# Forgetting attention: the causal masks of the diagonal blocks added in PSUM by VectorE instead of by TensorE products

## The chip, the core and the metric

The kernel runs on one core of one Trainium2 chip. The metric is device time in microseconds (us) of one launch. Engines: TensorE (PE; its weight loads are PEld), VectorE (DVE), ScalarE (ACT), GpSimd (POOL) and SyncE (SP). They run their own queues of instructions and meet through semaphores.

## The reference, cut to what matters

The program computes a chain of layers on a sequence of 1024 positions with 1024 channels in float32. The change touches one of them, the forgetting attention with 16 heads of 64 channels:

```
c = cumsum(log_f)                       # per head
logits[t, s] = q_t . k_s / sqrt(64) + c[t] - c[s]
mask = s <= t
probs = softmax(where(mask, logits, -inf))
out = probs @ v
```

Of a block of 128 queries, only the block of keys with the same positions (the diagonal block, 128 x 128) is cut by the mask; the keys before it are all seen, those behind it are never computed.

## The kernel before

The heads are done two at a time, eight pairs (p). `act_fox_pair`, `pe_fox_pair` and `dve_fox_pair` hold a pair's work for each engine; seven pairs run as a hardware loop (`Fori`), the eighth stands behind it. Every operand of a matrix product is split in a high and a low fp32r part, so that exact products take two or three passes.

A pair has two kinds of phases.

**Maximum phase, once for each head r.** For the eight blocks i of queries, TensorE computes the scores against the keys up to and with block i (`score`, line 2086, one product for each 512 columns) into one of two pairs of PSUM banks of psA, and adds the mask of the diagonal block with one more product of 128 columns (line 2088: identity times FHIDE, a 128 x 128 matrix that is large where the key lies behind the query). VectorE (`peak`, line 2407) adds the row of c and takes the minimum over all columns in one instruction; a second one reads the accumulator (READ) into NMX. It needs `fs_full` from TensorE; TensorE's score i+2 needs `fmax_ready` of peak i. After eight peaks TensorE turns the maxima (`row`, line 2095), and ScalarE writes them into a row of FX2 (line 2274).

**Sums, both heads.** The turned scores (keys on partitions) come in 24 pieces j of up to 512 queries. `PIECES` gives for each (r, h, n): head, half of the queries and block of keys. Where n >= 4h the piece begins at its diagonal block; those are pieces 0 to 7, 12 to 15 and 20 to 23, with widths 512, 384, 256, 128. For piece j: TensorE `turned` (lines 2111, 2112, and 2114, the mask product of 128 columns); ScalarE `exp` (2281) and `high` (2288); VectorE `low` (2413); TensorE `weigh` (2127, 2128 need the high part, 2130 the low part). The bank of piece j is reused by piece j+2, so TensorE's order is weigh(j), turned(j+2). The sums come out beside their denominators; `divide` (2423 reciprocals of 128 columns, 2430 and 2432 two multiplications) is spread over VectorE's queue by the table `DIVIDE`: behind low(5) to low(7), low(9) to low(13) and low(17) to low(21).

TensorE's order is written by hand: between these steps it works through slices of the next pair's projections (lines 321 to 323, three products of 512 columns a slice, into psG). `FILL_MAX` and `FILL_SUM` say how many slices stand ahead of each step, mostly one. In the last pair (`FILL_MAX_LAST`, `FILL_SUM_LAST`) the slices belong to the output projection, there are none ahead of the first six scores of head 0, and VectorE has low parts of that projection (line 999) between its peaks. GpSimd splits the weight tiles (lines 308, 310) when TensorE begins a tile, four times a pair.

`link` makes VectorE wait for its own instruction just issued (semaphore dve_step).

## Time and profile before

| | us |
|---|---|
| median of 3 runs | 2299.39 (2299.27 to 2303.89) |
| profiled execution, its own time | 2300.81 |
| its span in the profile | 2299.0 |
| mean granted TensorE clock, share of full speed | 0.981 |
| TensorE / VectorE / ScalarE / GpSimd busy | 2187.5 / 1205.1 / 861.0 / 551.7 |
| forgetting attention: seven looped pairs | 83.8 each |

The profile lists instructions with start and duration in us. A busy TensorE is not TensorE at its peak: durations of its products overlap, so what one costs is read from the starts. A bracket behind a row tells how long the engine was idle before it and what released it.

### The profile page before, as it was taken

What the parts mean: (1) busy time and instruction counts of PE and PEld (TensorE: products, weight loads), DVE (VectorE), ACT (ScalarE), POOL (GpSimd) and SP (SyncE); (2) the same over time, 40 slices, a digit from 0 to 9 for tenths busy, and PEclk for the clock granted to TensorE, in tenths of its full rate; (3) what the DMA queues carried; (4) which work ended last, traced back from release to release, by engine and by line L of the source; (5) the groups of instructions that cost most, each with busy time, mean ns of one, the idle gap of its engine ahead of it and who ended that gap; (6) DMA issues with size and microseconds to landing.
All of it is one profiled execution on the core that took longest, in us unless ns stands there. A gap on an engine that the chain in (4) does not pass through costs nothing.

```text
span 2299.0 us, 29340 instructions
## 1 busy us (share of the span) xinstructions
PE 2187.5 (95%) x11216; PEld 1852.2 (81%) x11216; DVE 1205.1 (52%) x1525; ACT 861.0 (37%) x1321; POOL 551.7 (24%) x292
## 2 busy tenths in 40 slices
PE   4899999999999899999899979999999999999996
PEld 4678888988888788898778868888888888877885
DVE  6963332453443634333435463566666667667734
ACT  3136554112022343323323123446546546544311
POOL 1322221323432122222233322111111111111520
PEclk9999999999999899999999989999999999999998
DMA  8112212111441211111131121111111011013201
GB/s 341 55 46 74 73 64 81 49 46 47 157 155 38 98 46 37 37 37 37 37 147 46 37 101 56 38 49 40 39 55 46 27 55 55 18 46 111 73 19 73
DMA packets 36661, 154.60 MB, mean 67 GB/s; under 512 B 4161, under 2 KB 4161, under 8 KB 35810
## 3 DMA queue, kind: packets, MB, share of 16 engines
q1 hardware_dynamic: 23840, 93.52, 11.7%
q10 hardware_dynamic: 12738, 59.87, 7.4%
q8 instruction: 64, 1.05, 0.2%
q14 instruction: 19, 0.16, 0.0%
HBM read 128.15 MB, written 21.04 MB: 65 GB/s over the span
## 4 chain that ended last, share of the span: by engine, by line
PE 84%; DVE 10%; issue 3%; ACT 2%; DMA 0%; DVEq 0%; SPq 0%; ACTq 0%
PE psG L321 22%; PE psG L323 21%; PE psG L322 21%; PE psA L2130 2%; PE psA L2112 1%; PE psA L2111 1%; PE psA L2128 1%; PE psA L2127 1%; PE psA L2012 1%; PE psA L321 1%; PE psA L2086 1%; PE psA L323 1%; PE psA L322 1%; DVE M L1043 1%; PE psA L2095 1%
## 5 line engine op out<-in xcount | busy, mean ns | idle before, releaser
L321 PE MATMUL psG<-AH,WH 128*128 128x512 f32 x2092 | 849.5, 406 | 39.2 <-DVE AL L999 12.3
L322 PE MATMUL psG<-AL,WH 128*128 128x512 f32 x2092 | 823.8, 394 | 0.0
L323 PE MATMUL psG<-AH,WL 128*128 128x512 f32 x2092 | 823.5, 394 | 0.0
L308 POOL TENSOR_SCALAR WH<-RAW 128x1024 fp32r<-128x1024 f32 x144 | 165.9, 1152 | 1659.9 <-PE psG L321 1183.3
L321 PEld LDWEIGHTS psG<-AH,WH 128*128 128x128 f32 x2092 | 398.1, 190 | 121.1 <-issue 26.4
L323 PEld LDWEIGHTS psG<-AH,WL 128*128 128x128 f32 x2092 | 397.1, 190 | 87.1
L322 PEld LDWEIGHTS psG<-AL,WH 128*128 128x128 f32 x2092 | 398.8, 191 | 68.3
L310 POOL TENSOR_TENSOR WL<-RAW,WH 128x1024 fp32r<-128x1024 f32 x144 | 386.0, 2680 | 12.0
L2413 DVE TENSOR_TENSOR FTL<-PF,FTH 128x512 fp32r<-128x512 f32 x192 | 112.8, 587 | 118.7 <-ACT FTH L2288 115.6
L2281 ACT ACTIVATE PF<-psA,PB 128x512 f32<-128x512 f32 x192 | 111.5, 581 | 81.2 <-PE psA L2114 45.6
L2423 DVE RECIPROCAL FDR<-psA 64x128 f32<-64x128 f32 x128 | 118.1, 939 | 32.1 <-PE psA L2130 30.5
L2407 DVE CUSTOM_DVE_ANT_0 JUNK<-psA,CB 128x128 bf16<-128x128 f32 (+7 forms) x128 | 96.7, 757 | 52.8 <-PE psA L2088 50.5
L321 PE MATMUL psG<-WH,AH 128*128 128x256 f32 x384 | 109.0, 284 | 0.0
L323 PE MATMUL psG<-WH,AL 128*128 128x256 f32 x384 | 108.7, 283 | 0.0
L322 PE MATMUL psG<-WL,AH 128*128 128x256 f32 x384 | 108.6, 283 | 0.0
L2288 ACT ACTIVATE FTH<-PF 128x512 fp32r<-128x512 f32 x192 | 100.8, 525 | 6.1
L1006 DVE TENSOR_TENSOR RS<-RS,SQ 128x1024 f32<-128x1024 f32 x38 | 70.3, 1850 | 34.4 <-ACT SQ L725 33.2
L725 ACT ACTIVATE SQ<-X 128x1024 f32<-128x1024 f32 x35 | 37.1, 1061 | 124.9 <-DVE X L1775 71.7
L322 PEld LDWEIGHTS psG<-WL,AH 128*128 128x128 f32 x384 | 73.7, 192 | 0.0
L321 PEld LDWEIGHTS psG<-WH,AH 128*128 128x128 f32 x384 | 73.7, 192 | 0.0
L323 PEld LDWEIGHTS psG<-WH,AL 128*128 128x128 f32 x384 | 73.7, 192 | 0.0
L713 ACT ACTIVATE AH<-Y 128x1024 fp32r<-128x1024 f32 x32 | 32.5, 1054 | 96.8 <-PE psG L323 78.1
(358 smaller groups left out, 3042.5 us busy)
## 6 DMA issues: line engine op xcount, KB each, us to landing
RAW<-w_tiles SPq DMA_DIRECT2D x144, 512.0 KB, 3.5
gates<-SIG ACTq DMA_DIRECT2D x16, 512.0 KB, 2.9
park<-X ACTq DMA_DIRECT2D x2, 4096.0 KB, 11.5
CB<-fox_c ACTq DMA_DIRECT2D x16, 512.0 KB, 4.4
X<-xT SPq DMA_DIRECT2D x4, 1024.0 KB, 12.1
WADA_SCALE<-w_ada SPq DMA_DIRECT2D x1, 4096.0 KB, 24.0
WADA_SHIFT<-w_ada SPq DMA_DIRECT2D x1, 4096.0 KB, 34.1
WADA_GATE<-w_ada ACTq DMA_DIRECT2D x1, 4096.0 KB, 16.4
```

Source lines behind the costliest of these rows:

```text
L308: nc.gpsimd.tensor_scalar(WH[:, i, :], RAW[:, i % RAW_SLOTS, :], 1.0, 0.0, ALU.mult, ALU.add).then_inc(w_high, 1)
L310: nc.gpsimd.tensor_tensor(WL[:, i, :], RAW[:, i % RAW_SLOTS, :], WH[:, i, :].bitcast(F32), ALU.subtract).then_inc(w_split, 1)
L321: first = nc.tensor.matmul(out, wh, xh, start=start, stop=False)
L322: nc.tensor.matmul(out, wh, xl, start=False, stop=False)
L323: return first, nc.tensor.matmul(out, wl, xh, start=False, stop=stop)
L1006: nc.vector.tensor_tensor(RS[:, :], RS[:, :], SQ[:, j % 2, :], ALU.add).then_inc(sq_used, 1)
L2130: nc.tensor.matmul(out, FVH[:, n, vs], FTL[:, j % 2, 0:w], start=False, stop=j in ENDS).then_inc(fpv_done, 1)
L2281: nc.scalar.activation(PF[:, j % 2, 0:w], psA[:, j % 2, 0:w], ACT.Exp, bias=PB[:, n, r:r + 1], scale=-1.0).then_inc(fexp_done, 1)
L2288: nc.scalar.activation(FTH[:, j % 2, 0:w], PF[:, j % 2, 0:w], ACT.Copy).then_inc(ft_high, 1)
L2407: nc.vector.tensor_tensor_reduce(out=JUNK[:, s % 2, 0:n], in0=pair((i + 1) % 2)[:, 0:n], in1=CB[:, r, 0:n], scale=1.0, scalar=3e38, op0=AL ...
L2413: nc.vector.tensor_tensor(FTL[:, j % 2, 0:w], PF[:, j % 2, 0:w], FTH[:, j % 2, 0:w].bitcast(F32), ALU.subtract).then_inc(ft_ready, 1)
L2423: l = nc.vector.reciprocal(FDR[hs, cs], psA[ds, 2 + r, cs])
```

## The change

- The mask product leaves `score` and `turned` (before: lines 2087, 2088, 2113, 2114).
- In `peak`, VectorE adds FHIDE (now plain float32) in place to the diagonal block in PSUM, waits for that addition with `link`, increments peak_begun, and then runs the reduction.
- In the sums, a new step `own(j)` of VectorE adds FHT, the other orientation of the mask, in place to the first 128 columns of the pieces in `OWN` (the 16 with a diagonal block) and signals `ft_masked`, for which `exp(j)` now waits. own(0) and own(1) stand ahead of low(0); own(j+2) stands behind low(j) and the first division step of that place.
- FHT is made once by VectorE from a constant matrix. Two semaphores f_min and f_ready become one. `chain.loop` keeps the count of the links within the loop.

```diff
@@ score (TensorE)
-                last = ks.stop == n
-                l = nc.tensor.matmul(out, FX[:, r, i * P:n], FKA[:, r, ks], start=True, stop=not last)
-                if last:
-                    l = nc.tensor.matmul(psA[:, 2 * b + i // 4, (i % 4) * P:(i % 4 + 1) * P], IDR[:, :], FHIDE[:, :], start=False, stop=True)
+                l = nc.tensor.matmul(out, FX[:, r, i * P:n], FKA[:, r, ks], start=True, stop=True)
@@ turned (TensorE)
-            l = nc.tensor.matmul(out, FKB[:, r, ks], FX2[:, r, qs], start=False, stop=lo > n * P)
-            if lo == n * P:
-                l = nc.tensor.matmul(psA[:, j % 2, 0:P], FHIDE[:, :], IDR[:, :], start=False, stop=True)
-            l.then_inc(ft_full, 1)
+            nc.tensor.matmul(out, FKB[:, r, ks], FX2[:, r, qs], start=False, stop=True).then_inc(ft_full, 1)
@@ exp (ScalarE)
-            act.wait_ge(ft_full, p * N_P + (j + 1))
+            if j in OWN:
+                act.wait_ge(ft_masked, p * len(OWN) + (OWN.index(j) + 1))
+            else:
+                act.wait_ge(ft_full, p * N_P + (j + 1))
@@ peak and own (VectorE)
+            own = psA[:, 2 * ((i + 1) % 2) + i // 4, (i % 4) * P:(i % 4 + 1) * P]
+            link(nc.vector.tensor_tensor(own, own, FHIDE[:, :], ALU.add))
             dve.sem_inc(peak_begun, 1)
...
+        def own(j):
+            if j in OWN:
+                dve.wait_ge(ft_full, p * N_P + (j + 1))
+                nc.vector.tensor_tensor(psA[:, j % 2, 0:P], psA[:, j % 2, 0:P], FHT[:, :], ALU.add).then_inc(ft_masked, 1)
@@ the sums of a pair (VectorE)
+        own(0)
+        own(1)
         for j in range(N_P):
             low(j)
-            for step in DIVIDE.get(j, ()):
+            steps = DIVIDE.get(j, ())
+            for step in steps[:1]:
+                divide(*step)
+            own(j + 2)
+            for step in steps[1:]:
                 divide(*step)
```

VectorE in the maximum phase, head 0, peaks 5 and 6, before (ISA with JUNK is the reduction, ISA with NMX alone the READ; the increment of peak_begun is not shown in such rows):

```order
L2400 REGISTER_ALU
L2407 ISA JUNK,NMX<-psA,CB 128x768 [waits fs_full,fmax_ready]
L2407 ISA NMX 128x1
L2400 REGISTER_ALU
L2407 ISA JUNK,NMX<-psA,CB 128x896 [waits fs_full,fmax_ready]
L2407 ISA NMX 128x1
```

The same place after the change:

```order
L2401 REGISTER_ALU
L2407 TENSOR_TENSOR psA<-psA,FHIDE 128x128 [waits fmax_ready,fs_full]
L228 REGISTER_ALU
L2410 ISA JUNK,NMX<-psA,CB 128x768 [waits dve_step]
L2410 ISA NMX 128x1
L2401 REGISTER_ALU
L2407 TENSOR_TENSOR psA<-psA,FHIDE 128x128 [waits fmax_ready,fs_full]
L228 REGISTER_ALU
L2410 ISA JUNK,NMX<-psA,CB 128x896 [waits dve_step]
L2410 ISA NMX 128x1
```

Each peak has one more VectorE instruction, and the reduction waits for VectorE's own semaphore instead of TensorE's.

VectorE in the sums, after the change, from the end of step j = 4 to low(7); before the change the rows of line 2416 are not there:

```order
L2416 TENSOR_TENSOR psA<-psA,FHT 128x128 [waits ft_full]
L2421 TENSOR_TENSOR FTL<-PF,FTH 128x384 [waits ft_high]
L2431 RECIPROCAL FDR<-psA 64x128 [waits fpv_done]
L2415 REGISTER_ALU
L2416 TENSOR_TENSOR psA<-psA,FHT 128x128 [waits ft_full]
L2431 RECIPROCAL FDR<-psA 64x128
L2421 TENSOR_TENSOR FTL<-PF,FTH 128x256 [waits ft_high]
L2431 RECIPROCAL FDR<-psA 64x128 x2
L2421 TENSOR_TENSOR FTL<-PF,FTH 128x128 [waits ft_high]
```

The additions are own(6) and own(7); they wait for TensorE, and low(5) and low(6) stand behind them.

VectorE at the end of a diagonal, from own(14) to low(14), after the change:

```order
L2416 TENSOR_TENSOR psA<-psA,FHT 128x128 [waits ft_full]
L2421 TENSOR_TENSOR FTL<-PF,FTH 128x384 [waits ft_high]
L2437 REGISTER_ALU [waits psum_free]
L2438 ISA [waits fdr_ready]
L2438 TENSOR_TENSOR FDR<-FDR,Y 64x512
L2439 REGISTER_ALU
L2440 TENSOR_TENSOR Y<-psA,FDR 64x512 [waits fdr_ready]
L2415 REGISTER_ALU
L2416 TENSOR_TENSOR psA<-psA,FHT 128x128 [waits ft_full]
L2421 TENSOR_TENSOR FTL<-PF,FTH 128x256 [waits ft_high]
```

own(14) and own(15), the two additions, stand ahead of low(13) and low(14).

## Rows read from the trace of the kernel before

**Rows 1.** The page: TensorE's busy time (part 1), the reductions (part 5).

```profile
PE 2187.5 (95%) x11216; PEld 1852.2 (81%) x11216; DVE 1205.1 (52%) x1525; ACT 861.0 (37%) x1321; POOL 551.7 (24%) x292
...
L2407 DVE CUSTOM_DVE_ANT_0 JUNK<-psA,CB 128x128 bf16<-128x128 f32 (+7 forms) x128 | 96.7, 757 | 52.8 <-PE psA L2088 50.5
```

**Rows 2.** Windows: second maximum phase and sums; from:to, us, busy (instructions), clock, DMA.

```profile
1622.50:1633.60 11.10, 10.67 (x53) 8.37 (x52) 7.33 (x18) 0.89 (x2) 3.46 (x2) 1.00 0.00 0
1634.30:1680.80 46.50, 46.42 (x243) 39.63 (x242) 28.68 (x42) 32.76 (x59) 4.66 (x3) 1.00 0.07 23
```

**Rows 3.** Timeline of TensorE around a mask product; start us, duration us, engine, line, operation.

```profile
1655.58 0.39 PE L2112 MATMUL psA<-FX,FKB 128*128 128x512 f32 x1
1655.80 0.22 PE L2114 MATMUL psA<-IDR,FHIDE 128*128 128x128 f32 x1
1655.86 0.45 PE L321 MATMUL psG<-AH,WH 128*128 128x512 f32 x1
1656.14 0.39 PE L322 MATMUL psG<-AL,WH 128*128 128x512 f32 x1
```

**Rows 4.** Timeline of the maximum phase, head 0.

```profile
1613.40 0.39 PE L2086 MATMUL psA<-FKA,FX 128*128 128x512 f32 x1
...
1613.63 0.22 PE L2088 MATMUL psA<-FHIDE,IDR 128*128 128x128 f32 x1
...
1614.07 0.69 DVE L2407 CUSTOM_DVE_ANT_0 JUNK<-psA,CB 128x512 bf16<-128x512 f32 x1 [0.47 <-PE psA L2088]
...
1618.85 1.23 DVE L2407 CUSTOM_DVE_ANT_0 JUNK<-psA,CB 128x1024 bf16<-128x1024 f32 x1 [0.16 <-DVE NMX L2407]
...
1620.00 0.08 DVE L2407 DVE_READ_ACCUMULATOR2_ANT NMX<- 128x1 f32 x1
...
1620.14 1.09 PE L2095 MATMUL psA<-MATS,NMX 128*128 128x128 f32 x8
```

**Rows 5.** Timeline of VectorE in the maximum phase, head 1: first reduction, last READ.

```profile
1624.63 0.28 DVE L2407 CUSTOM_DVE_ANT_0 JUNK<-psA,CB 128x128 bf16<-128x128 f32 x1
...
1633.37 0.08 DVE L2407 DVE_READ_ACCUMULATOR2_ANT NMX<- 128x1 f32 x1
```

**Rows 6.** Timeline of VectorE: a division, each operation waiting for the one before.

```profile
1604.34 0.95 DVE L2423 RECIPROCAL FDR<-psA 64x128 f32<-64x128 f32 x1
1605.43 0.69 DVE L2430 TENSOR_TENSOR FDR<-FDR,Y 64x512 f32<-64x512 f32 x1
1606.16 0.69 DVE L2432 TENSOR_TENSOR Y<-psA,FDR 64x512 f32 x1
```

**Rows 7.** Timeline of the sums: low(14), low(15), last product of weigh(14).

```profile
1662.00 0.43 DVE L2413 TENSOR_TENSOR FTL<-PF,FTH 128x256 fp32r<-128x256 f32 x1
...
1663.02 0.29 DVE L2413 TENSOR_TENSOR FTL<-PF,FTH 128x128 fp32r<-128x128 f32 x1 [0.59 <-ACT FTH L2288]
1663.07 0.28 PE L2130 MATMUL psA<-FTL,FVH 128*128 128x256 f32 x1
```

**Rows 8.** Timelines: VectorE beside GpSimd's subtraction, in three places.

```profile
1571.78 1.69 DVE L2413 TENSOR_TENSOR FTL<-PF,FTH 128x512 fp32r<-128x512 f32 x1
...
1653.91 2.81 POOL L310 TENSOR_TENSOR WL<-RAW,WH 128x1024 fp32r<-128x1024 f32 x1
1655.58 1.69 DVE L2413 TENSOR_TENSOR FTL<-PF,FTH 128x512 fp32r<-128x512 f32 x1
...
2116.40 2.40 POOL L310 TENSOR_TENSOR WL<-RAW,WH 128x1024 fp32r<-128x1024 f32 x1
2117.59 2.58 DVE L1775 TENSOR_TENSOR X<-X,psG 128x1024 f32<-128x1024 f32 x2
```

**Rows 9.** The last pair: first reduction, READ of the fifth; window 2036 to 2042.

```profile
2030.11 0.29 DVE L2407 CUSTOM_DVE_ANT_0 JUNK<-psA,CB 128x128 bf16<-128x128 f32 x1 [0.24 <-PE psA L2088]
...
2033.44 0.08 DVE L2407 DVE_READ_ACCUMULATOR2_ANT NMX<- 128x1 f32 x1
...
2036.00:2042.00 6.00, 4.47 (x15) 3.39 (x13) 5.43 (x5) 3.24 (x4) 3.96 (x2) 0.75 0.11 33
```

More of the change, by code:

```diff
@@ L1868, in build @@
     LFT, NCT = sb("LFT", [P, NB, FOX_HEADS], 220), sb("NCT", [P, NB, FOX_HEADS], 220.5)
-    FHIDE = sb("FHIDE", [P, P], 221, F32R)
+    FHIDE, FHT = sb("FHIDE", [P, P], 221), sb("FHT", [P, P], 222.3125)
     FREC = sb("FREC", [P, 2, 2 * NB], 221.5)
@@ L1878, in build @@
     SUMS_AT = HALF - 4 * NB
+    OWN = [j for j, (r, h, n) in enumerate(PIECES) if n >= 4 * h]
     FILL_MAX = [0, 1, 1, 1, 1, 1, 1, 1, 2, 0, 1, 2, 1, 1, 1, 1, 1, 1, 2]
@@ L1891, in build @@
     assert Q_AT[0] > filled(16) and K_AT[0] > filled(32)
-    f_min = sem("f_min")
     f_log = sem("f_log")
@@ L1922, in build @@
     fexp_done = sem("fexp_done")
+    ft_masked = sem("ft_masked")
     ft_high = sem("ft_high")
@@ L2028, in pe_fox_in @@
         gemm(pe, *fox_tile(0, 1))
-        pe.wait_ge(f_ready, 1)
+        pe.wait_ge(f_ready, 2)
         for n in range(NB):
@@ L2034, in pe_fox_in @@
         l.then_inc(f_turned, 1)
-        pe.wait_ge(f_ready, 2)
+        pe.wait_ge(f_ready, 3)
         for n in range(NB):
@@ L2245, in act_fox_gates @@
         fs = slice(0, FOX_HEADS)
-        act.wait_ge(f_min, 1)
+        act.wait_ge(f_ready, 1)
         nc.scalar.activation(EXF[fs, :], unit(U_F % 2)[fs, :], ACT.Abs, bias=col("b_f")[fs, :]).then_inc(psum_free, 1)
@@ L2370, in dve_fox_gates @@
         dve.wait_ge(psum_full, U_F + 1)
-        nc.vector.tensor_scalar(LF[fs, :], unit(U_F % 2)[fs, :], col("b_f")[fs, :], 0.0, ALU.add, ALU.min).then_inc(f_min, 1)
-        dve.wait_ge(f_min, 1)
+        nc.vector.tensor_scalar(LF[fs, :], unit(U_F % 2)[fs, :], col("b_f")[fs, :], 0.0, ALU.add, ALU.min).then_inc(f_ready, 1)
+        dve.wait_ge(f_ready, 1)
         dve.wait_ge(f_log, 1)
@@ L2376, in dve_fox_gates @@
         nc.vector.tensor_copy(LFT[:, :, :].rearrange("p n h -> p (n h)"), psA[:, 0, 0:NB * FOX_HEADS]).then_inc(f_ready, 1)
+        nc.vector.tensor_scalar(FHT[:, :], mat("causal_sum"), NEG, -NEG, ALU.mult, ALU.add)
         for r in range(2):
@@ L2474, in dve_fox @@
         with dve.Fori(0, PAIRS - 1) as p:
+            chain.loop(p, N_S)
             dve_fox_pair(dve, p, True)
+        chain.done(PAIRS - 1)
+        chain.loop(0, N_S)
         dve_fox_pair(dve, PAIRS - 1, False)
+        chain.done(1)
     def dve_final(dve, k):
```

## The prediction

> **What bounds the kernel now.** I read the page first: TensorE is busy 2187.5 of 2299.0 us, 95%; the times of VectorE's reductions stand in the same page [rows 1]. So each product that leaves TensorE is worth its issue time, as long as nothing else becomes the last thing that TensorE waits for. That is read from the stages the change touches. Seven of the eight head pairs repeat with a period of 83.8 us (the same long subtraction starts at 1571.78 and at 1655.58 [rows 8]). In the pair I read, TensorE has 0.43 us without work in the second maximum phase and 0.08 us in the 46.5 us of the sums [rows 2]: it is full. The timelines then show who is next. In the maximum phase the last reduction of head 0 is followed by the turning of the maxima 0.06 us after it ends (READ 1620.00 + 0.08, TensorE 1620.14), and TensorE had nothing left before that: VectorE ends this phase already [rows 4]. In the sums VectorE hands over its low part 0.64 us before TensorE wants it (1662.00 + 0.43 against 1663.07) [rows 7]. So the cover for new VectorE work is thin in both phases.
>
> **Removed: 256 mask products, 16 + 16 a pair.** A product of 128 columns does not cost its 0.22 us. The next one starts 0.06 us after it, and the one after that needs 0.28 us where the usual step is 0.23 (1655.80, 1655.86, 1656.14) [rows 3]. Together 0.115 us each: 16 x 0.115 = 1.84 us a phase kind and pair, 29 us over eight pairs if TensorE stayed full. The rest of the sum asks how much of it turns into waiting.
>
> **Added: 256 VectorE additions of 128 columns.** No addition in place in PSUM of this size is in the trace. The nearest rows are the subtraction of 128 columns, 0.29 us [rows 7], and the reduction whose time grows by 0.54 us for 512 more columns (0.69, 1.23) [rows 4], so 0.69 - 3 x 0.135 = 0.28 for 128. I take 0.29. When the next instruction waits for nothing, it starts about 0.08 us before the end of the one in front (1618.85 + 1.23 against READ at 1620.00), so an unbound addition takes 0.22 us of VectorE.
>
> **The link in the maximum phase.** The reduction now waits for its own addition, and between the two stands the increment of peak_begun, an instruction of the queue. VectorE handing over to itself costs 0.04 us when the wait is on the instruction (1605.43 + 0.69 to 1606.16) and 0.14 us when queue instructions stand in between (1604.34 + 0.95 to 1605.43) [rows 6]. From TensorE to a reduction behind such an increment it is 0.38 us (1613.63 + 0.06 to 1614.07) [rows 4], against about 0.22 without: 0.16 for the step. Bounds 0.04 and 0.20; I take 0.17, nearest to the two rows that have the queue instruction. Each peak then costs VectorE 0.29 + 0.17 = 0.46 us more.
>
> A rule of the Trainium skill speaks against this: "VectorE: DVE Perf Modes", in "The DRAIN you can't avoid", says that a semaphore after a VectorE operation costs nothing extra. By it an addition would take 0.22 us and a peak 0.22 more, the case C below. Rows 6 don't agree: with the semaphore the next operation comes 0.04 to 0.14 us after the end, not 0.08 before it.
>
> **Maximum phase, head 0.** Eight reductions of mean 0.757 us less 0.08 make 5.45 us [rows 1]. Score 3 starts at 1613.40 [rows 4] less three removed products, 1613.06; its 0.23 us and 0.22 us to VectorE put its addition at 1613.51. From here VectorE is never free: five peaks of 0.46 plus reductions of 512 to 1024 columns (mean 0.96 less 0.08, so 4.41 in all) end at 1613.51 + 2.30 + 4.41 + 0.08 = 1620.30, against 1620.08. So this phase gets 0.2 us longer, although TensorE has 0.9 us less to do.
> **Head 1.** VectorE takes its first score at 1624.63, right behind the low part of V [rows 5]. Now all eight peaks follow without a gap: 8 x 0.46 + 5.45 + 0.08 = 9.21, ending at 1633.84 against 1633.45: 0.4 us longer. Both: +0.6 us a pair. With a link of 0.04 the same working goes through slots that TensorE sets again and gives -0.7; with 0.20, +1.0.
>
> **Sums.** Piece j is turned by TensorE, masked by VectorE (own), exponentiated and split by ScalarE, its low part taken by VectorE, and weighed. The new order puts own(j+2) ahead of low(j+1), so low(j+1) now waits behind a piece that TensorE turns later. Take the end of a diagonal, pieces 14 and 22. From the end of turned(14) to the last product of weigh(14) TensorE has 2.38 us of work: two slices of 0.69, three products of 384 columns 0.53, the turning of 128 columns 0.23, two products of 256 columns 0.24. VectorE has 0.22 (handover) + own 0.22 + low(13) 0.49 (0.56 for 384 columns, between the rows for 256 and 512) + the two multiplications of the division 0.73 + 0.62 (0.69 each [rows 6], the first with its link of 0.04) + own 0.22 + low(14) 0.43 + 0.05 = 2.98 us. Stall 0.6 us, twice a pair. Piece 6, with two reciprocals (0.95 us each, 0.88 when queued) around own(7): 0.22 + 0.22 + 0.49 + 0.88 + 0.22 + 0.88 + 0.43 + 0.05 = 3.39 against the same 2.38: stall 1.0 us. Further handovers that are late by 0.03 to 0.15 us (pieces 0, 4, 8, 19 to 21) add 0.4. Piece 11 is late before and after: its subtraction is held until GpSimd's ends and takes 1.69 us [rows 8]. Sum: stalls 2.6 to 2.7, less 1.84 saved: +0.85 us a pair. With own at 0.22 instead of 0.29 (the short end) it is +0.3, with 0.36 or a handover of 0.30 it is +1.6.
>
> **The last pair.** It has no slices in front of the first scores, so VectorE runs from the first peak, whose addition can start 0.2 us before the reduction of 2030.11, since no queue instruction stands ahead of it: 2029.90 + 5 x 0.46 + the reductions of 128 to 640 columns (2.41) = 2034.61, against the READ of 2033.44: +1.2 after five peaks [rows 9], +1.7 after eight by the same steps; head 1 about +1.65 (four linked peaks pushed on, then TensorE's slices take some of it back); sums +0.85. After the idle stretch of this phase the granted clock stands at 0.75 in the window from 2036 to 2042 [rows 9], so between full speed and 1.2 GHz; a longer idle stretch prolongs that: 0 to 2 us, I take 1. Together +5.
>
> The setup outside the loop (one VectorE instruction for the second mask) lies beside TensorE's products and costs nothing; on the path it would be 0.3 us.
>
> **Sum.** 7 x (0.6 + 0.85) + 5 = 15 us. On the profiled execution, 2300.81 us with its span of 2299.0, that is 2316; the median of the runs is 1.4 us lower, 2299.39, which gives **2315 us**.
>
> **Rivals.**
> A, the forecast (0.62): VectorE is last in both phases, 2308 to 2322.
> B, the link is cheap (0.16): 0.04 us, as in the direct row of [rows 6]. Maximum phases -0.7, sums +0.3 to +0.85, last pair +1 to +3: 7 x (-0.4 to 0.15) + 2 = about 2300. Against it: the queue instruction is there in the order.
> C, faster (0.08): an addition takes 0.22 us of VectorE and hides in the gaps that VectorE has before most reductions (0.5 us at narrow widths, 0.2 at wide ones). Then both maximum phases shorten, 1.3 us a pair, and the sums lose only 0.2; 7 x -1.1, last pair -1: 2290. It decides at a peak cost of about 0.3 us; I have 0.46. The skill's rule above leads here.
> D, dearer (0.14): the additions are held while GpSimd subtracts, as the 1.69 us row was, or PSUM read and written in one instruction takes 0.36 us. Maximum +2.1, sums +1.6, last pair +8: 2333. Against the holding: two VectorE additions with one operand in PSUM ran at 1.29 us each within a GpSimd subtraction [rows 8].
>
> **How the numbers follow.** The point is A's. What a measurement of this kernel tells from no change is about 0.2%, 4.6 us, so 2295 to 2304. A and D lie above it, with B's upper edge: slower 0.77. Most of B: same 0.15. C: faster 0.08. The range leaves out C, B's lower edge and the far end of D: 2299 to 2331.
>
> **What would show it.** In the changed profile: reductions 0.17 us (0.04 to 0.20) behind the end of their additions; additions of 0.29 us; VectorE without a gap from peak 3 of head 0 and from peak 0 of head 1; TensorE idle before the turning of the maxima 1.2 us instead of 0.2; the low parts of pieces 6, 14 and 22 as releasers of weigh, by about 1.0, 0.6 and 0.6 us; a pair period of about 85.3 us instead of 83.8. A period below 83.8 would refute the account: TensorE's saving would then have survived. One above 87 would point to D.

## The result and the profile after

| | before | after |
|---|---|---|
| median | 2299.85 us (2299.27 to 2303.89) | 2339.64 us (2338.57 to 2340.77) |
| profiled span | 2299.0 | 2339.0 |
| mean granted clock | 0.981 | 0.974 |
| VectorE busy | 1205.1 | 1266.8 |
| TensorE busy | 2187.5 | 2193.7 |

The ratio is 1.017, 95% interval 1.0158 to 1.0182. The change is slower by 40 us; 15 were forecast, and 2339.6 lies above the range of 2299 to 2331. From the page after, engine use (the counterpart of the first line of [rows 1]) and the chain of work that ended last, and behind them the chain of the page before:

```profile
PE 2193.7 (94%) x10960; PEld 1830.2 (78%) x10960; DVE 1266.8 (54%) x1782; ACT 860.5 (37%) x1321; POOL 552.3 (24%) x292
PE 76%; DVE 15%; issue 6%; ACT 1%; DVEq 1%; DMA 0%; SPq 0%; ACTq 0%
...
PE 84%; DVE 10%; issue 3%; ACT 2%; DMA 0%; DVEq 0%; SPq 0%; ACTq 0%
```

VectorE's share of the chain grows from 10% to 15%.

TensorE has 256 products less and is not busy for a shorter time: a product that waits a little shows as a longer one, and products at 1.2 GHz last longer.

The useful cut is by pair, at five starts of TensorE instructions: the first score of head 0, the first turning of head 0's maxima, that of head 1's, the low product of piece 23, and the next pair's first score. The column "head 1" runs from the first turning to the second, "sums" from there to the low product of piece 23. Here and below, in us:

| looped pair | head 0 | head 1 | sums | to next pair | pair |
|---|---|---|---|---|---|
| before, all seven | 9.56 to 9.66 | 13.37 | 47.45 | 13.33 | 83.8 |
| after, from 1442.56 | 9.96 | 14.11 | 49.41 | 13.33 | 86.8 |
| from 1529.37 | 10.20 | 13.98 | 50.52 | 13.76 | 88.5 |
| from 1617.83 | 10.14 | 13.99 | 50.33 | 17.21 | 91.7 |
| from 1709.50 | 9.93 | 13.99 | 49.37 | 13.33 | 86.6 |
| from 1796.12 | 10.14 | 13.98 | 50.88 | 13.38 | 88.4 |
| from 1884.50 | 10.13 | 13.99 | 50.57 | 13.68 | 88.4 |
| from 1972.87 | 10.20 | 13.98 | 50.38 | 17.13 | 91.7 |

Two of seven pairs are whole at full clock: +2.8 to +3.1 us each. The other five are 1.7 to 5 us longer still, in the sums and behind them. The seven make +35.5 us, the last pair +4.9, what stands ahead of the pairs -0.5: the 40.

**Maximum phase after**, timeline of head 0 in the pair from 1796.12, the counterpart of [rows 4]:

```profile
1803.47 1.09 DVE L2410 CUSTOM_DVE_ANT_0 JUNK<-psA,CB 128x896 bf16<-128x896 f32 x1 [0.19 <-DVE psA L2407]
...
1804.49 0.08 DVE L2410 DVE_READ_ACCUMULATOR2_ANT NMX<- 128x1 f32 x1
1804.49 0.29 DVE L2407 TENSOR_TENSOR psA<-psA,FHIDE 128x128 f32<-128x128 f32 x1
...
1804.97 1.22 DVE L2410 CUSTOM_DVE_ANT_0 JUNK<-psA,CB 128x1024 bf16<-128x1024 f32 x1 [0.19 <-DVE psA L2407]
1806.12 0.08 DVE L2410 DVE_READ_ACCUMULATOR2_ANT NMX<- 128x1 f32 x1
...
1806.26 0.32 PE L2095 MATMUL psA<-MATS,NMX 128*128 128x128 f32 x1 [1.03 <-DVE NMX L2410]
```

The addition (L2407) starts with the READ, lasts 0.29 us, and the reduction follows 0.19 us behind its end. VectorE has no other gap, and TensorE stands idle 1.03 us for the last one; before, it came 0.06 us behind the READ without a stall to speak of.

**Sums after**, VectorE and TensorE around piece 6 in the pair from 1709.50:

```profile
1745.44 0.96 DVE L2431 RECIPROCAL FDR<-psA 64x128 f32<-64x128 f32 x1
...
1746.42 0.30 DVE L2416 TENSOR_TENSOR psA<-psA,FHT 128x128 f32<-128x128 f32 x1
...
1746.75 0.96 DVE L2431 RECIPROCAL FDR<-psA 64x128 f32<-64x128 f32 x1
...
1746.78 0.28 PE L2125 MATMUL psA<-FTH,FVL 128*128 128x256 f32 x1
...
1747.63 0.36 DVE L2421 TENSOR_TENSOR FTL<-PF,FTH 128x256 fp32r<-128x256 f32 x1
...
1748.04 0.39 PE L2127 MATMUL psA<-FTL,FVH 128*128 128x256 f32 x1 [0.98 <-DVE FTL L2421]
```

VectorE works through reciprocal, own(7), reciprocal and only then low(6), which TensorE wants from 1746.90 on. From 1746.78 to 1748.04 are 1.26 us where a product of 256 columns steps by 0.12: a stall of 1.14. Measured this way, the pair has 1.14 at piece 6, 0.81 at 14, 0.40 at 22, 0.37 at 11 (0.25 there before), and 0.04 to 0.16 at pieces 4, 13, 20 and 21.

**The clock.** TensorE at the end of the sums of the pair from 1617.83, then windows of the same stretch (from:to, us, then busy time and instructions of TensorE, its weight loads, VectorE, ScalarE, GpSimd, granted clock, DMA share, GB/s):

```profile
1687.11 0.38 PE L2127 MATMUL psA<-FTL,FVH 128*128 128x256 f32 x1 [0.25 <-DVE FTL L2421]
1687.33 1.84 PE L2015 MATMUL psA<-MATS,FSQ_Q 128*128 128x2 f32 x16
...
1690.06 0.40 PE L322 MATMUL psG<-AL,WH 128*128 128x512 f32 x1
1690.29 0.61 PE L323 MATMUL psG<-AH,WL 128*128 128x512 f32 x1
...
1691.12 0.63 PE L322 MATMUL psG<-AL,WH 128*128 128x512 f32 x1
```

```profile
1687.00:1689.00 2.00, 1.89 (x17) 1.89 (x17) 0.35 (x2) 1.93 (x4) 0.00 (x0) 1.00 0.00 0
1689.00:1690.00 1.00, 1.00 (x6) 0.86 (x6) 0.00 (x0) 0.00 (x0) 0.00 (x0) 1.00 0.00 0
1691.00:1699.00 8.00, 8.00 (x29) 7.05 (x29) 3.51 (x5) 1.31 (x2) 2.82 (x2) 0.50 0.34 127
```

Behind piece 22 TensorE computes the sums of squares of the next pair's queries: a row of products of two columns (L2015; below "the row"), 1.7 us in which it streams next to nothing. About 1 us behind it the 512-column products go from 0.40 to 0.63 us and the granted clock stands at 0.50, the 1.2 GHz level, for 10 us. A second such row, for the keys, stands behind piece 23; in this pair it lies within the 10 us:

```profile
1692.50 3.51 PE L2015 MATMUL psA<-MATS,FSQ_K 128*128 128x2 f32 x16
```

The clock fell in this place in five of seven looped pairs (from 1601, 1690, 1867, 1956 and 2045), for 3.4 us three times and for some 10 us twice: 31 us at half speed are 15.5 us lost. Both falls of 10 us contain all 16 products of the keys' row; those of 3.4 us contain none to four. The kernel before has no fall of the clock in its looped pairs.

### The profile page after: what moved, and what is told of

Read it like the earlier page. It is cut to its first block, busy times and chain, and to the rows that moved or that the text cites. A ratio compares the mean times of both kernels' runs of the same rounds, so it can differ in the third digit from the quotient of the medians.

```text
span 2339.0 us, 29414 instructions
## 1 busy us (share of the span) xinstructions
PE 2193.7 (94%) x10960; PEld 1830.2 (78%) x10960; DVE 1266.8 (54%) x1782; ACT 860.5 (37%) x1321; POOL 552.3 (24%) x292
## 3 DMA queue, kind: packets, MB, share of 16 engines
q8 instruction: 63, 1.03, 0.2%
## 4 chain that ended last, share of the span: by engine, by line
PE 76%; DVE 15%; issue 6%; ACT 1%; DVEq 1%; DMA 0%; SPq 0%; ACTq 0%
PE psG L321 20%; PE psG L323 19%; PE psG L322 19%; DVE FTL L2421 2%; PE psA L2127 2%; DVE FDR L2431 1%; PE psA L2015 1%; PE psA L2111 1%; PE psA L2112 1%; DVE psA L2407 1%; PE psA L321 1%; PE psA L323 1%; PE psA L322 1%; DVE M L1043 1%; DVE AL L999 1%
## 5 line engine op out<-in xcount | busy, mean ns | idle before, releaser
L323 PEld LDWEIGHTS psG<-AH,WL 128*128 128x128 f32 x2092 | 399.5, 191 | 87.2
L2421 DVE TENSOR_TENSOR FTL<-PF,FTH 128x512 fp32r<-128x512 f32 x192 | 106.9, 557 | 45.8 <-ACT FTH L2288 43.6
L2410 DVE CUSTOM_DVE_ANT_0 JUNK<-psA,CB 128x128 bf16<-128x128 f32 (+7 forms) x128 | 97.0, 758 | 24.4 <-DVE psA L2407 24.4
L2127 PE MATMUL psA<-FTL,FVH 128*128 128x512 f32 x192 | 76.0, 396 | 16.5 <-DVE FTL L2421 16.4
```

The costliest lines, as they stand in the source:

```text
L323: return first, nc.tensor.matmul(out, wl, xh, start=False, stop=stop)
L2127: nc.tensor.matmul(out, FVH[:, n, vs], FTL[:, j % 2, 0:w], start=False, stop=j in ENDS).then_inc(fpv_done, 1)
L2410: nc.vector.tensor_tensor_reduce(out=JUNK[:, s % 2, 0:n], in0=pair((i + 1) % 2)[:, 0:n], in1=CB[:, r, 0:n], scale=1.0, scalar=3e38, op0=AL ...
L2421: nc.vector.tensor_tensor(FTL[:, j % 2, 0:w], PF[:, j % 2, 0:w], FTH[:, j % 2, 0:w].bitcast(F32), ALU.subtract).then_inc(ft_ready, 1)
```

## Experiments

Theory A: the 40 us have two parts. VectorE comes last (20 us in the looped pairs, 5 in the last), and the waits this gives TensorE let the clock fall at the end of the sums (15.5). Rivals: the clock falls because of gaps anywhere, or because of something else in the change; and for the stalls of the sums, either VectorE's row of work or the ring through the low part makes them.

### Each phase alone, no masks, both

max_only keeps the product in the turned scores, sum_only that in the maximum phase; no_masks has neither products nor additions, that is, it leaves the masks out; both keeps all products and has all additions. The edit of max_only against the changed kernel:

```diff
-            nc.tensor.matmul(out, FKB[:, r, ks], FX2[:, r, qs], start=False, stop=True).then_inc(ft_full, 1)
+            l = nc.tensor.matmul(out, FKB[:, r, ks], FX2[:, r, qs], start=False, stop=lo > n * P)
+            if lo == n * P:
+                l = nc.tensor.matmul(psA[:, j % 2, 0:P], FHIDE[:, :], IDR[:, :], start=False, stop=True)
+            l.then_inc(ft_full, 1)
...
-        own(0)
-        own(1)
...
-            own(j + 2)
```

> VectorE adds the mask in the maximum phase alone; the turned scores keep their mask product on TensorE. Theory A (the cost has two parts: VectorE comes last, and the gaps that this leaves TensorE let the granted clock fall): from the first score product of a looped pair to the turning of head 0's maxima 9.95 us as in the full change (before 9.63), from there to head 1's 14.0 (before 13.37), the sums unchanged at 47.45; a looped pair 84.7 us where the clock is 1.00. That is 7 x 0.95 + 3.4 in the last pair = 10 us, 2310, and more only as far as windows of lower clock show beside it. Rival B (the clock falls only where several gaps follow each other closely, as in the sums): no lower clock at all here and 2310. Rival C (two gaps of 1 us a pair are enough): some 8 to 15 us more, 2318 to 2325.

> VectorE adds the mask to the turned scores alone; the maximum phase keeps its mask products. Theory A: maximum phases 9.63 and 13.37 us as before, sums 49.4 us (before 47.45) at a clock of 1.00, so 7 x 1.95 + 1.5 in the last pair = 15 us, 2315, plus what the granted clock costs. With rival B (the sums' gaps are what brings the clock down) the clock falls here as in the full change, 12 to 15 us more: 2327 to 2330. With rival C it falls in part.

> No mask products and no additions in their place: the causal masks of the attention are left out altogether (of the maxima and of the turned scores). It shows what the 256 products are worth. If TensorE is the bound everywhere, 256 x 0.115 = 29 us less: 2270, a looped pair 80.1 us. If VectorE and ScalarE already stand close behind it in the sums, less comes back: the sums 46.4 instead of 45.6 us, a pair 81, the whole 2277. The granted clock should stay where it was before (0.98).

> The additions on VectorE as in the change, and the mask products kept on TensorE too (each mask is added twice): VectorE's work of the change without TensorE's saving. If only VectorE's chain sets the pair (theory A), TensorE's products lie in gaps that are idle in the changed kernel where these are long, and show as 0.115 each elsewhere: a pair at full clock 0 to 1.5 us longer than the 86.7 of the change. If the gaps are what brings the clock down, they are shorter by up to 0.9 us each in the maximum phases here (0.1 to 0.2 instead of 1.03) and the clock falls less often: 2325 to 2335, at or below the full change's 2340 although there is more work. If the clock falls for another reason (VectorE's own work, say), 2340 to 2350.

| | median | ratio to before, interval | head 0 / head 1 / sums at full clock | pair |
|---|---|---|---|---|
| max_only | 2311.45 | 1.0047 (1.0033 to 1.0061) | 10.14 / 13.99 / 47.43 | 84.9 |
| sum_only | 2325.33 (2320.37 to 2339.86) | 1.0097 (1.0073 to 1.0121) | 9.6 / 13.37 / (50.2 to 51.7) | 87.2 to 92.0 |
| no_masks | 2276.02 | 0.9889 (0.9872 to 0.9905) | 8.90 / 12.63 / 45.73 | 80.6 |
| both | 2338.16 | 1.0159 (1.0142 to 1.0176) | 10.45 / 14.17 / 50.12 | 88.05 |

max_only came as theory A and rival B had it, and rival C is out: two stalls of 1 us a pair, and the clock stays at 1.00 over six of the seven looped pairs together (the first has no fall either):

```profile
1530.00:2039.00 509.00, 493.30 (x2544) 408.97 (x2543) 360.03 (x649) 277.52 (x444) 85.00 (x48) 1.00 0.14 43
```

sum_only has the clock falls, in every looped pair of the profiled execution, so no pair of it is at full clock throughout; its four runs lie between 2320 and 2340, since the number and length of the falls differ from run to run. Its median of 2325 is just short of the 2327 to 2330 of rival B, and its falls are what that rival said: the stalls of the sums suffice, without those of the maximum phases. no_masks gives what the products are worth: 0.73 us in each maximum phase and 1.72 in the sums, 3.2 a pair and 24 us in all, not 29. Its whole came as the lower of the two gains expected, its sums (45.73) as the higher. Set against it, the additions cost 1.03 to 1.24, 1.36 and 3.64 us a pair. Its narrow pieces are as bare of mask products as the change's, and over its looped pairs but the first the clock stays at 1.00, so the missing products alone don't bring the clock down:

```profile
1526.00:2009.00 483.00, 477.14 (x2447) 399.77 (x2446) 337.18 (x553) 276.93 (x444) 85.05 (x48) 1.00 0.14 45
```

both missed its expectation. At full clock its pairs are 1.4 us longer than the change's, near the upper end of what was expected; its clock fell in two looped pairs (at 1692 and 1958) instead of five. Fewer falls and more work nearly cancel: 2338.

### Is it the idle time in the sums?

filler issues products with a block of zeros (512 columns, 0.23 us each) in the stalls; VectorE's work stays as changed.

```diff
+            for _ in range({6: 5, 11: 1, 14: 3, 22: 1}.get(j, 0)):
+                nc.tensor.matmul(psA[:, 2 + r, 0:HALF], FVH[:, n, vs], FVL[:, :, HD:2 * HD], start=False, stop=False)
             pe.wait_ge(ft_ready, p * N_P + (j + 1))
```

> The full change, and in the sums TensorE computes products with a block of zeros, added to the output that piece 6, 11, 14 or 22 is being added to, where it would else stand idle for the low part: 5, 1, 3 and 1 products of 0.23 us (idle there: 1.14, 0.37, 0.81 and 0.40). VectorE's work and its order are the change's. If the idle itself is what lets the granted clock fall (theory A), the looped pairs keep a clock of 1.00: each 86.7 to 87.3 us, and the whole 2326 instead of 2340. If the clock falls for another reason, nothing moves or the zero products add their own time: 2340 to 2343, with the 1.2 GHz windows where they were.

2336.26 us (2334.03 to 2339.21), ratio 1.0154 (1.0137 to 1.0171). The stalls are filled: at full clock a pair takes 86.6, as without them. Four stretches at 1.2 GHz are left (from 1602, 1779, 1868 and 1957, for 10, 3, 3 and 10 us), 27 us instead of 31 in five. So idle time at pieces 6, 11 and 14 isn't what brings the clock down, and theory A's second half fell in this form. What the falls have in common is their place: each begins between the second half of the row and 1.1 us behind its end, which led to the experiments on the row.

### The stalls of the sums: VectorE's row of work, or the ring

moved takes division steps away from in front of low(6), low(14) and low(22). early issues turned(j+2) ahead of the low product of piece j, so that turned(j+2) and own(j+2) no longer wait for low(j). The expectation below says this of the exponential and the high part too; that is not so. They still wait for buffers of piece j: the exponential for low(j) (ft_ready, line 2280 of the changed kernel), the high part for its low product (fpv_done, line 2287). So early shortens the ring and doesn't cut it. early_moved has both. before_early is early's move in the kernel before.

```diff
-    DIVIDE = {5: [(0, 0, 0), (0, 0, 1)], 6: [(0, 0, 2), (0, 0, 3)], 7: [(0, 0, 4)]}
-    DIVIDE.update({9 + step: [(1, 0, step)] for step in range(5)})
-    DIVIDE.update({17 + step: [(0, 1, step)] for step in range(5)})
+    DIVIDE = {5: [(0, 0, 0)], 6: [(0, 0, 1), (0, 0, 2)], 7: [(0, 0, 3), (0, 0, 4)]}
+    DIVIDE.update({(9 + step, 15)[step == 4]: [(1, 0, step)] for step in range(5)})
+    DIVIDE.update({(17 + step, 22)[step == 4]: [(0, 1, step)] for step in range(5)})
```

```diff
         def weigh(j):
...
+            if j + 2 < N_P:
+                turned(j + 2)
             pe.wait_ge(ft_ready, p * N_P + (j + 1))
             nc.tensor.matmul(out, FVH[:, n, vs], FTL[:, j % 2, 0:w], start=False, stop=j in ENDS).then_inc(fpv_done, 1)
...
             weigh(j)
-            if j + 2 < N_P:
-                turned(j + 2)
```

> The full change with the divisions' steps on VectorE in other places: the reciprocals (0,0,0) at piece 5, (0,0,1) and (0,0,2) at 6, (0,0,3) and the two products at 7; the two products of (1,0) behind piece 15 instead of 13, of (0,1) behind 22 instead of 21. The stalls before the low products of pieces 6, 14 and 22 (1.14, 0.81 and 0.40 us) are put down to VectorE's row of work ahead of these low parts; if that is right they go or fall under 0.3, and new ones of up to 0.5 us come at 7, 8, 16 and 23: the sums 47.8 to 48.8 us instead of 49.4, and the clock falls less often, 2320 to 2332. If the ring (low part, low product, turned product, addition, exponential, high part, low part) sets the pace, the stalls stay whatever VectorE does between: the sums 49.2 to 49.8, 2335 to 2342.

> The full change with one move on TensorE: the two turned score products of piece j+2 are issued before the low product of piece j instead of behind it, so that addition, exponential and high part of j+2 no longer hang on the low part of j. The sum of TensorE's own work in the sums is 45.7 us (the run without masks). If the ring through the low part makes the stalls, they go but for what VectorE's own row of work leaves at pieces 6, 14 and 22: the sums 46.0 to 47.4 us, no lower clock in the looped pairs, a pair of 83.5 to 84.7 us, the whole 2300 to 2310. If VectorE's row alone makes them, only the 0.46 us of the two products is hidden at each: the sums 48.0 to 48.8 us, the whole 2318 to 2332.

> The full change with both moves: the divisions' steps in their other places and the turned products of piece j+2 ahead of the low product of piece j. If the stalls of the sums have two causes that add up (VectorE's row of work at pieces 6, 14 and 22, worth 1.35 us a pair by the run moved, and the ring through the low part, worth 1.95 by the run early, of 3.65 us over TensorE's own 45.7), the sums are 46.1 to 46.9 us, a pair 83.6 to 84.2, the whole 2301 to 2308. If both moves cure the same stalls, 47.3 us and 2309 to 2314.

> The kernel before with the same move alone (turned products of piece j+2 ahead of the low product of piece j, mask products kept). If TensorE is the bound of the sums there, the move gives nothing: sums 47.3 to 47.5 us, 2299 to 2301.

| | median | ratio to before, interval | sums at full clock | pair |
|---|---|---|---|---|
| moved | 2317.90 | 1.0076 (1.0059 to 1.0093) | 48.02 | 85.5 |
| early | 2321.65 (2315.04 to 2342.22) | 1.0112 (1.0057 to 1.0168) | 47.41 | 84.8 |
| early_moved | 2303.20 | 1.0011 (1.0001 to 1.0020) | 46.30 | 83.75 |
| before_early | 2296.15 | 0.9981 (0.9971 to 0.9990) | 47.07 | 83.4 |

What ended TensorE's idle time in one pair of moved (us in all, times, longest):

```profile
PE psA L2095 <- DVE NMX L2410: 2.1, 2, 1.0
PE psA L2124 <- DVE Y L2440: 0.7, 1, 0.7
PE psA L2088 <- DVE FVL L2452: 0.5, 1, 0.5
PE psA L2127 <- DVE FTL L2421: 0.2, 1, 0.2
```

In the changed kernel the low parts (FTL) stand in that list with 2.1 us in four waits; here 0.2 are left. The new wait of 0.7 is at piece 8, the first of the second half of head 0, which needs the output bank that the moved division (Y) still reads:

```profile
1741.83 0.50 PE L2124 MATMUL psA<-FTH,FVH 128*128 128x512 f32 x1 [0.68 <-DVE Y L2440]
```

Net 1.35 us less: the sums came as expected (47.8 to 48.8), the stalls of the row went. early gives 1.96 less, at the end of the 46.0 to 47.4 expected, and early_moved 3.07 of 3.64 us, as expected of two causes that add up (3.31). Where they take it shows when the start of the last slice ahead of each piece, and that of the row, is set against the same start in no_masks, both counted from the turning of head 1's maxima. What a run gets later there from one piece to the next, in us, one pair each (the other pairs agree within 0.05):

| pieces | 0 to 5 | 6 | 7, 8 | 9 to 11 | 12, 13 | 14 | 15 to 21 | 22 | all |
|---|---|---|---|---|---|---|---|---|---|
| after | 0.39 | 1.08 | 0 | 0 | 0.20 | 0.90 | 0.54 | 0.50 | 3.6 |
| moved | 0.34 | 0.14 | 1.08 | 0 | 0.20 | 0 | 0.54 | 0 | 2.3 |
| early | 0.04 | 0.43 | 0.26 | -0.47 | 0.05 | 0.45 | 0.18 | 0.67 | 1.6 |
| early_moved | 0.01 | -0.19 | 1.08 | -0.46 | 0.05 | -0.06 | 0.18 | -0.07 | 0.5 |

VectorE's row of work at pieces 6, 14 and 22 makes 2.5 of the 3.6 us. moved takes nearly all of that and gets 1.1 back at piece 8. The other 1.1 us lie in many small handovers; moved leaves them, and early takes 0.9 of them: that is the ring. The rest of early's gain is not plainly the ring's: 1.1 us at pieces 6 and 14, where turned(j+2) now stands ahead of the low product and fills part of the stall, and 0.5 at piece 11, where the low part is late in the kernel before too [rows 8]. It loses 0.4 at pieces 8 and 22.

before_early was expected to give nothing and gave 0.38 us a pair. By the same working it gains 0.40 at piece 11, and the other places cancel: the sums of the kernel before weren't bound by TensorE alone either.

early, moved and early_moved also bear on the clock. It falls in two, one and none of the looped pairs; early's runs spread from 2315 to 2342, against the 2300 to 2310 without falls that were expected of it. But the length of the stall right ahead of the row doesn't decide alone, since early's at piece 22 is longer than the change's (the change first, then early):

```profile
1778.52 0.39 PE L2127 MATMUL psA<-FTL,FVH 128*128 128x256 f32 x1 [0.24 <-DVE FTL L2421]
...
1852.29 0.38 PE L2129 MATMUL psA<-FTL,FVH 128*128 128x256 f32 x1 [0.48 <-DVE FTL L2421]
```

### The row of two-column products

spread issues the row of the queries two blocks at a time with three slices between, and leaves the keys' row as it is; before_double issues the row twice in the kernel before; gap22 and gap10 let VectorE do two idle reductions ahead of low(22) or low(10) in the kernel before; late_fill puts six products of zeros into the stall at 22 and into the row of the changed kernel.

```diff
@@ before_double
                 pe_fox_sums(pe, nxt, 0)
+                pe_fox_sums(pe, nxt, 0, False)
...
@@ gap22 (gap10: j == 10)
         for j in range(N_P):
+            for x in range(2 if more and j == 22 else 0):
+                nc.vector.tensor_reduce(SCR[:, x:x + 1], FX[:, x, :].bitcast(F32), mybir.AxisListType.X, ALU.add)
             low(j)
@@ late_fill (zeros(): one product of zeros, 512 columns)
+            if more and j == 22:
+                for _ in range(2):
+                    zeros()
             pe.wait_ge(ft_ready, p * N_P + (j + 1))
...
-                pe_fox_sums(pe, nxt, 0)
+                pe_fox_sums(pe, nxt, 0, zeros)
```

> The full change; only the issue order on TensorE at the end of the sums differs: the 8 sums of squares of the next pair's queries (16 matmul records of two columns, 1.7 us in a row behind piece 22) are issued two at a time, with the three slices of full-width products that followed them between. The granted clock fell in the looped pairs within some us of that row (at 1601, 1690, 1867, 1956 and 2045 us), and filling the idle time ahead of it did not help. If a long row of two-column products behind short stalls is what precedes the fall, it falls less or not at all: pairs of 86.7 us, 2325 to 2328. If the row has nothing to do with it, the falls stay: 2336 to 2342.

> The kernel before with the same row of two-column products issued twice (their results are the same again, and told once). No stall is added, TensorE goes on working. 1.7 us more a pair by itself: 7 x 1.7 = 12, 2312, a pair of 85.5 us. If a long stretch of such products is enough to bring the clock down, the looped pairs show 1.2 GHz windows behind it and the pairs are 87 to 90 us: 2320 to 2345. If it takes stalls besides, the clock stays at 1.00 in the pairs.

> The kernel before (mask products, no additions); in each looped pair VectorE does two reductions of 1024 columns into an unused buffer ahead of the low part of piece 22, so that TensorE stands idle 1 to 1.5 us right before the row of two-column products. By itself 7 x 1.3 = 9 us: 2309. If a stall there is what brings the clock down, 1.2 GHz windows begin within 5 us behind it in most pairs, and the whole is 2320 to 2345. If the change's falls have to do with its additions, the clock stays at 1.00 in the looped pairs.

> The same two reductions ahead of the low part of piece 10, twelve pieces before the row of two-column products, among pieces of 512 columns; TensorE idle 1.2 to 2 us there. By itself 7 x 1.6 = 11 us: 2308 to 2314, with no 1.2 GHz window in the looped pairs, if it takes the stall next to the row. If idle time anywhere counts, windows of lower clock come here as in gap22.

> The full change with 6 products of zeros over 512 columns more a pair on TensorE: two in the stall at piece 22, and one behind every second block of the row of squares. They cost up to 6 x 0.23 less the stall of 0.4: 1.0 us a pair. If what matters is how little TensorE streams around that row, the clock stays at 1.00 in the looped pairs: 87.7 us each, 2331 to 2334, faster than the change although there is more work. If products of zeros don't count (which would also explain the run filler), the falls stay: 2345 or more.

| | median | ratio to before, interval | falls in looped pairs | pair |
|---|---|---|---|---|
| spread | 2333.71 | 1.0145 (1.0128 to 1.0162) | 5, of 3.4 us each | 86.6; 88.3 with a fall |
| before_double | 2332.44 | 1.0140 (1.0123 to 1.0157) | 7 | 87.1, then 88.8 |
| gap22 | 2329.93 | 1.0121 (1.0104 to 1.0139) | 6 | 85.4 to 91.8 |
| gap10 | 2310.97 | 1.0045 (1.0029 to 1.0062) | 0 | 85.3 |
| late_fill | 2332.41 | 1.0137 (1.0120 to 1.0154) | 0 | 87.8 |

gap22 and gap10, the wait in one pair each and windows at the stall and behind it, gap22 first:

```profile
PE psA L2130 <- DVE FTL L2413: 1.4, 1, 1.4
```

```profile
1771.00:1775.00 4.00, 2.62 (x18) 2.25 (x16) 3.48 (x6) 2.54 (x5) 0.00 (x0) 1.00 0.00 0
1777.00:1787.00 10.00, 10.00 (x34) 8.74 (x35) 2.48 (x4) 1.31 (x2) 3.41 (x2) 0.50 0.24 70
```

```profile
PE psA L2130 <- DVE FTL L2413: 1.6, 1, 1.6
```

```profile
1742.00:1748.00 6.00, 4.39 (x22) 3.38 (x21) 5.91 (x7) 2.74 (x5) 2.38 (x1) 1.00 0.26 87
1768.00:1780.00 12.00, 12.00 (x74) 10.50 (x74) 7.68 (x10) 3.43 (x4) 3.40 (x2) 1.00 0.24 87
```

The same idle time, 1.4 and 1.6 us: next to the row the clock falls in six of seven pairs, twelve pieces earlier in none; 19 us lie between the two kernels. VectorE's additions aren't needed for a fall. Nor is any stall; before_double, the doubled row (no idle time stands before it) and windows over its beginning and from within it on:

```profile
1773.33 4.55 PE L2012 MATMUL psA<-MATS,FSQ_Q 128*128 128x2 f32 x32
...
1771.00:1775.00 4.00, 4.00 (x31) 3.76 (x29) 1.70 (x4) 2.89 (x6) 0.00 (x0) 1.00 0.00 0
1776.00:1781.00 5.00, 5.00 (x17) 4.32 (x18) 0.00 (x0) 0.00 (x0) 1.02 (x1) 0.50 0.00 0
```

TensorE is "busy" 4.00 of 4.00 us, and the clock falls in the middle of the row. In the other direction late_fill came as expected: six products more than the change, all stalls of pieces 6 and 14 still there, and behind the row

```profile
1778.00:1784.00 6.00, 6.00 (x38) 5.29 (x38) 1.98 (x3) 1.08 (x2) 3.40 (x2) 1.00 0.03 12
1784.00:1797.00 13.00, 13.00 (x67) 10.75 (x66) 11.85 (x20) 7.69 (x8) 2.09 (x2) 1.00 0.51 156
```

with 7 us off the whole although each pair at full clock is 1.2 us longer. So products of zeros, two in the stall at 22 and four within the row, take the falls away, where filler's one at 22 and nine elsewhere didn't. Which of the six are needed wasn't tried.

spread came between its two expectations (2325 to 2328, 2336 to 2342). It deals out only the queries' row. All its falls begin at the end of the keys' row, still whole, or up to 1.1 us behind it, as in this pair, where the clock falls at 1693:

```profile
1690.40 1.89 PE L2015 MATMUL psA<-MATS,FSQ_K 128*128 128x2 f32 x16
```

They hold at most two two-column products, and all are short. What precedes each fall is a stretch from the narrow pieces 20 to 22 to one of the two rows, in which few columns are streamed, and in the changed kernel a stall besides. In the kernel before the same stretch, with its mask products and no stall, passes without a fall.

### A version faster than both

hybrid is early_moved with VectorE's additions in the maximum phase only where it waits for TensorE anyway: peaks 0 to 2 of head 0.

```diff
...
-                l = nc.tensor.matmul(out, FX[:, r, i * P:n], FKA[:, r, ks], start=True, stop=True)
+                last = ks.stop == n and (r or i > 2)
+                l = nc.tensor.matmul(out, FX[:, r, i * P:n], FKA[:, r, ks], start=True, stop=not last)
+                if last:
+                    l = nc.tensor.matmul(psA[:, 2 * b + i // 4, (i % 4) * P:(i % 4 + 1) * P], IDR[:, :], FHIDE[:, :], start=False, stop=True)
...
-            link(nc.vector.tensor_tensor(own, own, FHIDE[:, :], ALU.add))
+            if not r and i < 3:
+                link(nc.vector.tensor_tensor(own, own, FHIDE[:, :].bitcast(F32), ALU.add))
```

> As early_moved, and in the maximum phase VectorE adds the mask only in the peaks 0, 1 and 2 of head 0, where it waits for TensorE anyway; the other 13 keep the mask product. Expected of head 0: 9.3 us to the turning of its maxima (before 9.63), of head 1 13.37 as before, sums 46.1 to 46.9, the seam 13.33: a pair of 82.2 to 82.9, faster than before (83.78): 2287 to 2294. If the additions in the narrow peaks hold the later ones after all, head 0 is 9.6 to 9.8 and the whole 2292 to 2297.

2289.73 us (2288.10 to 2290.26), ratio 0.9953 (0.9936 to 0.9969): faster than before by 10.6 us, than the change by 50. Head 0 takes 9.42, head 1 13.37, the sums 46.27, a pair 82.4. It came as expected, but for head 0 (9.3 expected). TensorE's waits in one pair, and the clock over the looped pairs but the first (1.00):

```profile
PE psA L2127 <- DVE Y L2444: 0.8, 1, 0.8
PE psA L2089 <- DVE FVL L2456: 0.4, 1, 0.4
```

```profile
1526.00:2019.00 493.00, 485.26 (x2522) 407.89 (x2521) 363.19 (x665) 275.44 (x444) 84.53 (x48) 1.00 0.14 44
```

Part of this is early's move, which is worth 0.38 us a pair without any addition. With it, 16 additions in place of products in the sums, and the divisions moved, are worth 0.8 us a pair more (47.07 to 46.27), the three narrow peaks 0.2 (9.64 to 9.42). The divisions moved without any addition were not run, so how much of the 0.8 the additions bring stays open.

## Why the prediction was wrong

**Held.** The bound and who is next: TensorE is full before, VectorE last after the change. The cost of an addition: 0.29 taken, 0.295 and 0.298 us measured. The link: 0.17 taken, 0.19 measured in 128 reductions (24.4 us in all), inside 0.04 to 0.20; so cases B and C fell. What of the 0.19 is the increment of peak_begun wasn't tried apart. The Trainium skill ("VectorE: DVE Perf Modes", "The DRAIN you can't avoid") says that a semaphore after a VectorE operation costs nothing extra, which led to C. This trace doesn't agree for an instruction that waits for that semaphore: the reduction starts 0.19 us behind the addition's end. VectorE has no gap from peak 3 of head 0 on. TensorE is idle before the turning of the maxima for 1.03 us; 1.2 were named. The stalls stand at pieces 6, 14 and 22, as 1.14, 0.81 and 0.40 against 1.0, 0.6 and 0.6. The last pair: +4.9 against +5, with some luck in the parts: +1.7, +1.7 and +1.5 in head 0, head 1 and the sums, against 1.7, 1.65, 0.85 and 1 for the clock; what the clock took of them (10 us at 1.2 GHz, before 7) wasn't separated. D fell: no addition was held by GpSimd, and the pairs above 87 us, which were to point to D, come from the clock.

**Mis-sized: the maximum phases.** +0.2 and +0.4 were taken; at full clock it is +0.3 to +0.5 and +0.62 (max_only: 10.14 - 9.63 and 13.99 - 13.37). A pair +0.9 to +1.1 instead of +0.6, some 3 us in all, at the bound of +1.0. The same working with the measured link of 0.19 gives 0.1 more over the five bound peaks of head 0 and 0.16 over the eight of head 1: most of the difference in head 1, and a third or more of it in head 0. (A slip of the working is too small to matter: eight times 0.757 less 0.08 is 5.42, not 5.45.)

**Mis-sized: the sums.** +0.85 was taken, 0.3 to 1.6 allowed; +1.92 came, 7.5 us more over seven pairs. Two terms failed. What the products are worth is 1.72, not 1.84 (no_masks). And the stalls are 3.64 us, not 2.6. The prediction laid out VectorE's row of work ahead of low(6), low(14) and low(22): 2.2 forecast, 2.5 found in the table by pieces above. It did not lay out the ring: low(j), low product, turned(j+2), own(j+2), exponential, high part, low(j+2). The addition lengthens it by 0.3 us and a handover in the own pieces. "Further handovers that are late by 0.03 to 0.15 us", taken as 0.4, was this ring, counted at a few pieces: 1.1 us came, and early takes 0.9 of them. This is the term of the sums that was most mis-sized.

**Left out: the granted clock in the looped pairs.** This is the large miss, 15.5 of the 25 us. The prediction read the clock only in the last pair, where a window showed 0.75 [rows 9], and gave it 1 us there. For the looped pairs it had no term and no rival; the windows of [rows 2] showed 1.00 there, and it asked no further. The row of two-column products behind the narrow pieces was in the code and in the trace, but how near the clock was to a fall there was never asked. With sizes as measured at full clock the sum is 7 x 2.9 + 4.9 - 0.5 = 24.7, that is 2324, inside the range; the clock took it out.

**The account of 40 us:** maximum phases 7 x 1.0 = 7, sums 7 x 1.9 = 13.3, clock 15.5, last pair 4.9, ahead of the pairs -0.5.

What stays open is how the falls are dealt among pairs: five of seven here, seven in sum_only, six in gap22, and not the same from run to run. Nor was the stall at piece 22 taken away alone in the changed kernel: late_fill puts products into it and into the row at once, and moved takes away the stalls at 6 and 14 with it. So how much of the 15.5 us hangs on that stall, and how much on the rest of the stretch, isn't shown.

## What to carry to other kernels

Before moving work from a full engine to an idle one, lay out the row of work of the engine that gets more, and follow each buffer once around its ring as well: here the row cost 2.5 us a pair and the ring's small handovers 1.1, of which 0.4 had been seen. Take the moved work only where the receiving engine waits anyway (three peaks of sixteen), and move first what stands between a buffer's release and its refill. And look for stretches where TensorE is busy with products that stream few columns: a stall beside one (gap22) made the kernel 19 us slower than a like stall elsewhere (gap10).

## What the hardware showed that was not expected

- The granted clock went to the 1.2 GHz level within a row of 32 two-column products that TensorE worked through without idle time (before_double; 1773.33 to 1777.88, the fall at 1775.8); 1.6 us of idleness among 512-column products (gap10) and two stalls of 1 us a pair (max_only) left it at 1.00.
- The falls came in lengths of 3.4, 6.8, 10 and 13.7 us (after, before_double, gap22), without idle time of TensorE in them. Those of 3.4 us hold none to four two-column products, those of 6.8 us 13, of 10 us 16, and of 13.7 us 21 and 25. In the stretches of 512-column products a product took 0.63 us.
- With six products of a block of zeros added around the row (late_fill) the clock stayed at 1.00, so such products do count.
- A short wait lengthens a product's row instead of showing as idle time: at piece 6, of the 1.14 us of stall, 0.98 stand in the bracket, and the product itself shows 0.39 us where its neighbour of the same 256 columns shows 0.28. The waits of 0.04 to 0.16 us at other pieces stand in no bracket at all.
